# The last six modulation columns move from TensorE, in the heads of the second block, to VectorE, in its output projection; modulation slots of the context projection change places

## The reference, cut to what matters

```python
def trunk_layer(x, ctx, c_act, cc_act, w_mod, b_mod, ...):
    mod = (c_act @ w_mod + b_mod)[:, None, :]
    mod_c = (cc_act @ w_mod + b_mod)[None, None, :]
    sh1, sc1, gt1, sh2, sc2, gt2 = jnp.split(mod, 6, axis=-1)
    csh1, csc1, cgt1, csh2, csc2, cgt2 = jnp.split(mod_c, 6, axis=-1)
    h = rmsnorm(x, g_norm1) * (1 + sc1) + sh1
    hc = rmsnorm(ctx, g_norm1) * (1 + csc1) + csh1
    ...
    x = x + gt1 * merge_groups(...)
    h2 = rmsnorm(x, g_norm2) * (1 + sc2) + sh2
    x = x + gt2 * conv_ffn(h2, ...)
```

## Time and profile before

| What | Value |
|---|---|
| Median of three runs | 2389.2 us (2386.78 to 2389.31) |
| Profiled execution, its time and span | 2390.77 us, 2389.0 us |
| Busy: PE, DVE, ACT | 2357.9 (99%), 1669.9 (70%), 1130.1 us (47%) |
| Chain that ended last | PE 94%, DVE 3%, ACT 2%, issue 1% |
| PE waits for VectorE's `wlo` (L649) | 5.1 us in 6 waits |
| DMA | 532.78 MB, mean 223 GB/s |

### The profile page before, as it was taken

One profiled execution on the slowest core, in us unless ns is written; L12 is line 12 of the kernel. 1 busy time (PEld: TensorE's weight loads), 2 busy tenths in 40 slices (PEclk: granted clock), 3 DMA queues, 4 the chain that ended last, 5 costly groups with the idle time before them and its releaser, 6 DMA issues.

```text
span 2389.0 us, 30857 instructions
## 1 busy us (share of the span) xinstructions
PE 2357.9 (99%) x11910; PEld 1998.6 (84%) x11910; DVE 1669.9 (70%) x2060; ACT 1130.1 (47%) x1401; POOL 0.2 (0%) x4
## 2 busy tenths in 40 slices
PE   8999999999999999999999999999999999999998
PEld 7888888888888888887788888788888888888887
DVE  5445778868877877657558764576788667885786
ACT  5444555444445445555355443454534434443444
POOL 0000000000000000000000000000000000000000
PEclk9999999999999999999999999999999999999999
DMA  8552677777877777567639954254555565555554
GB/s 298 194 193 89 253 262 278 298 284 275 299 280 289 288 271 298 179 190 308 237 117 366 341 190 166 106 150 168 193 186 192 193 207 192 186 193 194 187 187 146
DMA packets 137059, 532.78 MB, mean 223 GB/s; under 512 B 19232, under 2 KB 19360, under 8 KB 124016
## 3 DMA queue, kind: packets, MB, share of 16 engines
q1 hardware_dynamic: 136656, 531.07, 63.2%
q10 hardware_dynamic: 288, 0.11, 0.0%
HBM read 529.02 MB, written 2.11 MB: 222 GB/s over the span
## 4 chain that ended last, share of the span: by engine, by line
PE 94%; DVE 3%; ACT 2%; issue 1%; DMA 0%; DVEq 0%; SPq 0%; ACTq 0%
PE PSA L827 23%; PE PSA L649 18%; PE PSA L650 18%; PE PSA L651 18%; PE PSA L823 6%; PE PSA L830 6%; PE PSA L869 1%; DVE wlo L1933 0%; DVE u L2070 0%; PE PSA L1155 0%; ACT whi L1328 0%; PE PSA L772 0%; DVE QZ L2230 0%; PE PSA L1016 0%; PE PSA L894 0%
## 5 line engine op out<-in xcount | busy, mean ns | idle before, releaser
L1933 DVE TENSOR_TENSOR wlo<-raw,whi 128x1024 fp32r<-128x1024 f32 x788 | 933.4, 1218 | 375.6 <-ACT whi L1328 374.4
L1328 ACT ACTIVATE whi<-raw 128x1024 fp32r<-128x1024 f32 x788 | 800.3, 1052 | 496.0 <-DMA raw<-in_w_down 180.7
L827 PE MATMUL PSA<-u,whi 128*128 128x512 f32 x2368 | 566.1, 391 | 0.0
L827 PEld LDWEIGHTS PSA<-u,whi 128*128 128x128 f32 x2368 | 435.1, 188 | 84.2 <-DVE u L2070 0.2
L649 PE MATMUL PSA<-whi,u 128*128 128x512 f32 x1088 | 426.1, 392 | 6.1 <-DVE wlo L1933 5.1
L650 PE MATMUL PSA<-wlo,u 128*128 128x512 f32 x1088 | 423.5, 389 | 0.0
L651 PE MATMUL PSA<-whi,u 128*128 128x512 f32 x1088 | 423.5, 389 | 0.0
L649 PE MATMUL PSA<-whi,ahi 128*128 128x512 f32 x856 | 333.4, 389 | 0.0
L651 PE MATMUL PSA<-whi,alo 128*128 128x512 f32 x856 | 333.0, 389 | 0.0
L650 PE MATMUL PSA<-wlo,ahi 128*128 128x512 f32 x856 | 333.0, 389 | 0.0
L649 PEld LDWEIGHTS PSA<-whi,u 128*128 128x128 f32 x1088 | 204.3, 188 | 51.6 <-DVE wlo L1933 5.0
(11 more groups left out here) (331 smaller groups left out, 1334.2 us busy)
## 6 DMA issues: line engine op xcount, KB each, us to landing
raw<-in_w_up SPq DMA_DIRECT2D x300, 512.0 KB, 3.7
raw<-in_w_in SPq DMA_DIRECT2D x208, 512.0 KB, 4.4
raw<-in_w_down SPq DMA_DIRECT2D x192, 512.0 KB, 4.2
mod_slot<-in_w_mod_rows SPq DMA_DIRECT2D x90, 1024.0 KB, 6.0
raw<-in_w_out SPq DMA_DIRECT2D x64, 512.0 KB, 4.3
raw<-in_w_down2b SPq DMA_DIRECT2D x20, 512.0 KB, 3.7
raw<-in_w_mod SPq DMA_DIRECT2D x12, 512.0 KB, 3.3
c_all<-in_c_rows SPq DMA_DIRECT2D x2, 1024.0 KB, 4.6
```

The lines of the kernel that those rows point to most:

```text
L827: mm = pe.matmul(both, wh[:, c], u_pair[:, k, :], start=k == 0, stop=k == KD - 1)
L1328: AF(whi[:, n % SLOTS, 0:w], raw[:, n % SLOTS, 0:w], ACT.Copy).then_inc(hi_done, 1)
L1933: TT(wlo[:, n % SLOTS, 0:w], raw[:, n % SLOTS, 0:w], whi[:, n % SLOTS, 0:w], ALU.subtract).then_inc(lo_done, 1)
```

## The change

1. The three `Fill` units in the heads go, with their 12 tile loads, 48 matmuls on TensorE, 3 copies on ScalarE, 6 tiny matmuls and 3 additions on VectorE, and with them the constant `sel`, the columns of `c` in `vec` and the first ScalarE function `Silu` on `cst`.
2. Columns 90 to 95 are made by VectorE in blocks 1 and 2 (of 0 to 3) of `out2`: six loads of 1 MB, six `mod_sum`, a new load of `c` (1 MB), its `Silu` on ScalarE with a `Sqrt` table put back behind it, and one addition of biases.
3. In `inC` the two slots lie at other places, so that the first load waits only for `nar_done`, and the second alone for `gate_done`.
4. In `inL` the `Silu` of `c` moves from ahead of the second turn to behind its second tile.
5. `gt2` is stored in `up2_0` and loaded in `dn2_0`.
6. In the heads, tiles that lie over `whi` change halves, since the ring starts at another slot; TensorE's wait for `kt_exp` moves to the end of the levels.

```diff
-GLA_UNITS = 3
+FOR_OUT2 = 6
-VEC = [("g_mix", KD), ("g_mlp", KD), ("g_n1", KD), ("g_n2", KD), ("c", KD), ("cc", KD), ("b_mod", NMODCH),
+VEC = [("g_mix", KD), ("g_mlp", KD), ("g_n1", KD), ("g_n2", KD), ("b_mod", NMODCH),
...
-    ph.append(Fill("heads", GLA_UNITS))
-    ph.append(Phase("out2", "tok", 2, 2, 8, k=KD, evac="gres"))
+    ph.append(Phase("out2", "tok", 2, 2, 8, k=KD, evac="gres", mods=SINGLES, mod_blocks=(1, 2)))
...
-        mod_slots3 = [z_at(f"mod_slot3{n}", [P, D], F32, (24 + 8 * n) * K) for n in range(2)]
+        mod_slots3 = [z_at(f"mod_slot3{n}", [P, D], F32, (32 - 8 * n) * K + 64) for n in range(2)]
+        mod_slots4 = [z_at(f"mod_slot4{n}", [P, D], F32, 8 * n * K) for n in range(2)]
+        c_all4 = z_at("c_all4", [P, D], F32, 16 * K)
...
-                if p.name == "inC":
+                if p.name == "inC" and b == 0 and j == 0:
+                    sp.wait_ge(B["nar_done"], 1)
+                if p.name == "inC" and b == 0 and j == 1:
                     sp.wait_ge(B["gate_done"], 1)
...
+            def c_for_out2():
+
+                sp.wait_ge(tp_ready, 40)
+                load(c_all4[:, :], t_in["c_rows"][0].partition_broadcast(P), "c")
...
+                            if p.name == "out2" and (i, b, t) == (0, 1, 0):
+                                c_for_out2()
...
                 if p.name == "out2":
                     sp.wait_ge(B["mo_add"], 4)
                     load_gate(0)
-                    sp.wait_ge(mini_done, BY["out2"].unit0)
+                if p.name == "up2_0":
+                    sp.wait_ge(gate2_done, 1)
                     store_gate(1, 5 * KD)
-                if p.name == "up2_0":
+                if p.name == "dn2_0":
                     sp.wait_ge(acc_free, BY["up2_0"].blk0)
                     load_gate(1)
...
-                if lev == 1:
-                    pe.wait_ge(B["kt_exp"], 2)
-                if 1 <= lev <= GLA_UNITS:
-                    if lev >= 2:
-                        mod_columns(5, heads.unit0 + lev - 2, apart=True)
-                    fill_tiles(heads, lev - 1, 4)
...
+            def c_silu_for_out2():
+                act.wait_ge(ld["c"], 64)
+                AF(c_all4[:, :], c_all4[:, :], ACT.Silu).then_inc(c_silu, 1)
+                root_table(3)
...
+                            if p.name == "inL" and i == 1 and (b, t) == (0, 1):
+                                c_silu_again()
+                            if p.name == "out2" and (i, b, t) == (0, 1, 1):
+                                c_silu_for_out2()
...
-                        if p.name == "inL" and i == 1:
-                            c_silu_again()
...
             def start():
                 act.wait_ge(ld["vec"], 16)
-                AF(cst[:, 0:2 * KD].rearrange("p (k w) -> p w k", w=2),
-                   vec[:, OFF_V["c"][0]:OFF_V["c"][0] + 2 * KD].rearrange("p (w k) -> p w k", w=2), ACT.Silu).then_inc(silu_done, 1)
...
+                            if p.name == "out2" and (i, b, t) == (1, 1, 0):
+                                add_biases(BY["up2_0"].mod0, BEFORE_OUT2, NMODCH, 1).then_inc(gate2_done, 1)
...
-                         2: lambda: mod_adds(5, heads.unit0),
-                         3: lambda: mod_adds(5, heads.unit0 + 1),
-                         4: lambda: (chunk_ends(), last_columns()),
+                         4: lambda: (chunk_ends(), value_ones()),
```

More of the change, by code:

```diff
@@ L42 @@
 GROUPS1 = 4
-UNIT = 4
-GLA_UNITS = 3
-UW = TW // UNIT
 PAIRS = ((0, 2, (1, 2)), (3, 2, (4, 6)))
@@ L103, in cuts, with with_mods @@
         return [1] + ([self.mods_to] if self.mods and 1 < self.mods_to < self.iters else []) + ([ROWS_HIGH] if self.name == "inL" else []) + [self.iters]
-    def with_mods(self, i, part):
+    def with_mods(self, i, part, b):
         if not self.mods:
             return False
+        if self.mod_blocks:
+            return i * self.blocks + b in self.mod_blocks
         if isinstance(i, int):
@@ L175, in plan @@
         p.mod0, p.both0, p.single0 = mods, both, single
-        times = (p.mods_to - p.mods_from) * p.blocks
+        times = len(p.mod_blocks) if p.mod_blocks else (p.mods_to - p.mods_from) * p.blocks
         mods += times * len(p.mods)
@@ L651, in product @@
                 return pe.matmul(dst, xl, wh, start=False, stop=stop)
-            def mod_tile(bank, slot, n, t):
-                pe.wait_ge(arrived[slot], n)
-                for j in range(4):
-                    k = UNIT * t + j
-                    mm = pe.matmul(PSA[32 * j:32 * j + 32, bank, 0:UW], cst[:, 2 * k:2 * k + 32], raw[:, slot, j * UW:(j + 1) * UW],
-                                   start=t == 0, stop=t == UNIT - 1)
-                mm.then_inc(tile_used, 1)
[L662 to L666, removed]
-                for c in range(2):
-                    mm = pe.matmul(PSA[:, bank, UW + 2 * c:UW + 2 * c + 2], modrow[:, c * P:(c + 1) * P], cA("sel"), start=True, stop=True)
-                mm.then_inc(mini_ready, 1)
-            def fill_tiles(f, u, bank):
-                for t in range(UNIT):
-                    q = f.seq0 + UNIT * u + t
-                    mod_tile(bank, q % SLOTS, 16 * (q // SLOTS + 1), t)
             def narrow(x, part):
@@ L1119, in _ @@
                     transposed(7, 0, B["mt_ready"])
-                if lev == 4:
-                    mod_columns(5, heads.unit0 + 2, apart=True)
                 if lev == 5:
@@ L1937, in mod_sum @@
                 m = p.mod_no(b, j)
-                slot = {"inC": mod_slots3, "inL": mod_slots2}.get(p.name, mod_slots)[m % 2]
+                slot = {"inC": mod_slots3, "inL": mod_slots2, "out2": mod_slots4}.get(p.name, mod_slots)[m % 2]
                 col = p.mod_col(i, b, j)
@@ L1942, in mod_sum @@
                     dve.wait_ge(mod_here[m % 2], p.counted(16 * (m // 2 + 1), i, 8 * p.mods_per_iter))
-                    dve.wait_ge(c_silu, 2 if p.name == "inL" else 1)
+                    dve.wait_ge(c_silu, {"inL": 2, "out2": 3}.get(p.name, 1))
                     if m:
@@ L2304, in heads2 @@
                         doubled(4 * 2 ** lev)
-                    after[lev]()
+                    if lev in after:
+                        after[lev]()
                 dve.wait_ge(B["gc_done"], 1)
```

106 lines of the change are left out of this document (33 added, 73 removed).

## The result

| What | Before | After |
|---|---|---|
| Median | 2389.31 us (2386.78 to 2390.95, 5 runs) | 2402.3 us (2401.74 to 2402.95, 5 runs) |
| Ratio, 95% interval | | 1.0055 (1.0044 to 1.0065) |
| Profiled execution: time, span | 2390.77 us, 2389.0 us | 2402.3 us, 2400.5 us |

What follows compares the result with a forecast made beforehand. TensorE was taken as the bound (94% of the chain of waits). The terms +1.3 + 3.4 - 1.5 - 0.8 - 0.3 = +2.1 us on the median 2389.2 us gave 2391.3 us, range 2386.2 to 2394.5 us.

Steps and rivals of the forecast that it cites:

- the reading of the change part by part: Step through the start, `inC`, `inL`, heads, `out2` and the clock, giving each a term in us.
- The start, +1.3 us: Kernel start: ScalarE's first table load now waits for `tp_ready`, so TensorE starts at 12.6 instead of 11.32 us.
- the rival that it doesn't wait: Kernel start: the first table load does not wait, so nothing is lost there; 2386.6 us, chance 0.07.
- The clock at the start, +3.4 us: Kernel start: after a 2.54 us pause TensorE's clock falls, about 7 us at 0.51 losing 3.4 us; bounds 0 and 3.4.
- `inC`, -1.5 us: `inC`: tiles issued before the wait for the gates remove TensorE's 1.47 us wait; the 0.59 us wait stays.
- `inL`, -0.8 us: `inL`: the later `Silu` removes TensorE's 0.81 us wait; the third tile may keep 0.2, so -0.6 to -0.8 us.
- The heads, -0.3 us: Heads: VectorE bounds the levels, so dropped matmuls give nothing; three dropped additions give 0.2 to 0.5 us, taken as 0.3.
- The clock in the heads, 0: Heads: the 1.75 us wait and the fall behind it stay; taken as 0, bounds -3.4 and +3.4 us.
- The slower rival: Heads: the clock falls on the path too, 3.4 us more; 2394.7 us, or 2396.0 with slower transposes; chance 0.10.
- `out2`, 0: `out2`: the added sums, loads and `Silu` fit beside TensorE's work, with a slack of 5 us; no cost.
- the rival without a fall: Kernel start: TensorE's clock does not fall after the longer pause; 2387.9 us, chance 0.30.
- The clock term: Kernel start: the +3.4 us for a fall of TensorE's clock behind the longer pause, called the most doubtful term.

Runs made afterwards that it cites:

- z128_table: `z128` plus a `Silu` on one column of `vec` as ScalarE's first function, ahead of any wait; 2386.18 us, ratio 0.9986 to the kernel before.
- z128: The changed kernel with 128 bytes of padding before Z, so `ahi` and `alo` lie as before the change; 2388.95 us, ratio 0.9999 to the kernel before.
- ring0: The changed kernel with the weight ring, `whi` and `u` moved up 384 bytes to multiples of 512, and Z 128 past one; 2406.50 us, one run.
- z128_old_waits: `z128` with `inC`'s first modulation load waiting on `gate_done` again and `inL`'s `Silu` of `c` ahead of its second turn; 2389.76 us, one run.
- z256: The changed kernel with 256 bytes of padding before Z, so `ahi` and `alo` lie 256 past a multiple of 512; 2402.47 us, one run.
- z64: The changed kernel with 64 bytes of padding before Z, so `ahi` and `alo` lie 64 past a multiple of 512; 2395.79 us, one run.
- z384: The changed kernel with `levels` cut by 128 unused bytes, so `ahi` and `alo` lie 384 past a multiple of 512; 2387.08 us, one run.
- u_off: The changed kernel with 128 bytes of padding ahead of `u`, moving `u` against `whi` and Z back to 128 modulo 512; 2413.92 us, one run.
- before_z0: The kernel before with `levels` cut by 128 unused bytes, so Z, `ahi` and `alo` lie as after the change; 2403.87 us, ratio 1.0061.

## Why the prediction was wrong

**The step that failed** is the reading of the change part by part. Item 1 of the change names "the columns of `c` in `vec`" and `sel` as removed, and the prediction gave that removal no term; it held that "all the change can do at these places is a handful of pauses of 0.1 to 3 us". The removal moved Z by 128 bytes and with it the held operands of 2568 products, from a distance of 0 to one of 128 modulo 256 to the streamed ones. These cost 14.5 us (5.65 ns each), more than all terms of the sum together. No row of the trace of before could price it, since it had no product with such operands. But the size of the exposure could be read: 2568 products of `ahi` and `alo`, a quarter of TensorE's time. A range that owned up to this would have been wider.

**The start, +1.3 us:** right in mechanism, measured +1.13 us. The load carried the wait, and the rival that it doesn't wait has fallen: it ran at 7.97 us, and in `z128_table`, with a function ahead of the wait, at 1.69 us. That one trace came so near is partly luck, since the first product moves by about 1 us between executions: against the kernel before it came 0.29 to 1.24 us later in the eight kernels with the late load (mean 0.83), and 0 to 1.00 us earlier in the five without it (mean 0.48). The difference of the means is 1.3 us.

**The clock at the start, +3.4 us:** mis-sized. In the profile after it was 0, in `z128` 1.51 us. The error is in "7 us at 0.51 lose 3.4 us": the fall lasted 3.41 us in four of the five traces that had one, and even the one of 6.83 us, in `ring0`, cost only 2.8 us, because it began in the pause. Over the eight traces the mean loss is 1.1 us. And the length of the pause doesn't decide alone. The clock fell behind pauses of 1.82, 1.88, 2.51, 2.67 and 2.75 us (`z128_old_waits`, `z256`, `z128`, `z64`, `ring0`) and stayed full behind 1.58 us (after, `z384`) and behind 2.83 us (`u_off`):

```profile
12.42 0.47 PE L640 MATMUL PSA<-whi,u 128*128 128x512 f32 x1 [2.83 <-DVE wlo L1872]
```

```profile
11.00:20.00 9.00, 7.58 (x41) 6.39 (x42) 6.03 (x9) 4.61 (x11) 0.00 (x0) 1.00 1.02 415
```

That half of the chances went to a fall fits five traces of eight; that its full price went into the sum does not. The Trainium skill (TensorE: Matmul & The Clock Gate, "What's actually happening") says that the engine's warm-up varies from run to run of one kernel. The traces agree: the changed kernel and `z128` begin with the same instructions, and their clock first rose at 11.2 and at 8.3 us.

**`inC`, -1.5 us:** right in mechanism, measured -1.93 and -1.99 us. The term took the listed idle time of the wait; a wait costs more than that, since the idle time begins where the product before it ends (0.39 us behind its start, though the next could start after 0.23) and the first products behind it are 0.1 us slow. The wait of 0.6 us stayed, as said.

**`inL`, -0.8 us:** the low end was nearer: -0.47 to -0.55 us. What is late next is the third tile, as said, but by 0.38 us instead of at most 0.2.

**The heads, -0.3 us:** 0.16 us with the clock alike. VectorE stayed the bound.

**The clock in the heads, 0:** right for the change, wrong as a picture. The fall is no fixed cost: its part on the path was 6.83 us before and 3.41 us in `before_z0`, and 6.83, 3.41 or 0 us in kernels with the change. The slower rival (a second fall on the path) did not come; a second fall came, in a level, and was free.

**`out2`, 0:** right. TensorE waits there once, 0.87 us at its head, as before. The `Silu` ran at 1592.5 us and six sums of 2.28 us fit beside the products.

Without the move of Z the time would have lain in the range, but not at the forecast: the trace of `z128` is 0.2 us shorter than the one of the kernel before, where 2.1 us more were forecast. The clock term was 1.9 us too large for it, the gain of `inC` 0.5 us too small, and the start 0.7 us too large. Its median, 2388.95 us against 2390.0 us, is nearer to the rival without a fall (2387.9 us) than to the forecast of 2391.3 us, though its trace had a fall.

## What to carry to other kernels

Where a change adds, removes or resizes a tile, list the start addresses of all TensorE operands before and after, and count the products whose two operands change their distance modulo 256 bytes. At 128 bytes off, each product of 512 columns cost 5.5 to 5.7 ns more here, or 4.3 ns in the MLPs' up projections; other shapes and types were not tried, but for 256 columns. Fix such places with an explicit offset or an assert, so that an unrelated tile can't move them. Judge a small gain only after comparing the same product's start in both traces, stretch by stretch; the busy totals and the medians mix it with falls of the clock that come and go.

## What the runs showed of the hardware

- A fp32r product (the type of the rounded halves) of 128x128 held by 512 streamed columns came every 226.7 ns when its two operands in SBUF lay a multiple of 256 bytes apart, and every 232.4 ns at 128 bytes off; at 64 bytes off the mean was about 2 ns above the fast one, with two of three groups slower and one not. The products with `whi` held and `u` streaming came every 228.6 and 232.8 ns. With no other engine and no DMA at work the loss was the same. It made no difference at which multiple of 128 the pair lay, or which of the two had moved. Products of 256 columns were not slowed (165 to 167 us for 1184 of them in all kernels, `u_off` with its distance of 128 included).
- A table load as ScalarE's first instruction ahead of a wait cost nothing (at 1.69 us in `z128_table`), and behind it 1.28 us (at 7.97 us in the changed kernel), with no drain to be seen: the function follows 0.02 us later.
- Falls of TensorE's clock to half (1.2 GHz) lasted 3.41 or 6.83 us in all traces here (the low clock behind the last product, at the end of each trace, apart). Where TensorE had work at hand they cost 1.4 to 1.8 us and 2.8 to 3.3 us.
